# Output stage of a diffusion step's expert retrieval: the low part of V of odd experts on GpSimd, that of even ones on VectorE

## The reference, cut to what matters

```
def expert_block(args):                      # idx, g: the 128 chosen experts of a token and their gates
    hx, ix, gx = args
    act = jax.nn.gelu(jnp.einsum('tkd,td->tk', u_tab[ix], hx))
    return jnp.einsum('tk,tkd->td', gx * act, v_tab[ix])
...
x = x + g2 * peer(h, *peer_w)
y = rmsnorm(x, lnf_w)
```

## Time and profile before

| | us |
|---|---|
| three runs | 3542.67, 3549.48, 3549.56 |
| median | 3549.48 |
| span of the profiled execution, first to last instruction | 3542.8 |
| steady part of the output stage, within it | 2476 to 3466 |
| TensorE busy, whole span | 3304.0 (93%) |
| VectorE busy, whole span | 2784.9 (79%) |
| GpSimd busy, whole span | 1444.2 (41%) |
| ScalarE busy, whole span | 1255.0 (35%) |
| gathers of the output stage (L1859), 372 | 543.1 on GpSimd |
| adding their rows (L1880), 372 | 457.1 on VectorE |

### The profile page before, as it was taken

The page is one execution under the profiler, slowest core; times in us unless marked ns, Lnnn a source line. Parts: engine busy times, 40 slices in busy tenths (PEclk is TensorE's granted clock), DMA queues, the critical chain, the costliest instruction groups (busy, mean ns, idle before and its releaser), DMA issues. The chain is left out here.

```text
span 3542.8 us, 50319 instructions
## 1 busy us (share of the span) xinstructions
PE 3304.0 (93%) x17854; PEld 2976.8 (84%) x17854; DVE 2784.9 (79%) x4757; ACT 1255.0 (35%) x2299; POOL 1444.2 (41%) x950
## 2 busy tenths in 40 slices
PE   5999969699799999999699999997999999999997
PEld 2989959554799999999699999997888888888886
DVE  4555237597477799999888888884799999999998
ACT  2331135333322222222577777773222222222221
POOL 0000012111111377787555555542455655555550
PEclk8999979899899999999899999998999999999999
DMA  5235324542111377777699999996999999999993
GB/s 183 93 131 175 113 88 153 192 137 89 49 38 40 121 264 234 241 254 252 250 381 345 345 344 346 345 332 246 328 366 375 365 366 359 378 361 365 371 362 157
DMA packets 379005, 880.27 MB, mean 248 GB/s; under 512 B 32530, under 2 KB 198946, under 8 KB 375682
## 3 DMA queue, kind: packets, MB, share of 16 engines
q1 hardware_dynamic: 256004, 390.58, 33.6%
q0 software_dynamic: 115600, 423.31, 32.2%
q10 hardware_dynamic: 7280, 65.01, 4.6%
HBM read 740.61 MB, written 138.18 MB: 248 GB/s over the span
## 5 line engine op out<-in xcount | busy, mean ns | idle before, releaser
L1859 POOL DMA_INDIRECT hT<-peer_v,hT x372 | 543.1, 1460 | 448.8 <-DVE hrow L1880 333.9
L1719 PE MATMUL ps<-h_hi,u_hi 128*128 128x384 f32 x2048 | 696.0, 340 | 23.0 <-POOL u_lo L1601 15.2
L1719 PE MATMUL ps<-h_lo,u_hi 128*128 128x384 f32 x2048 | 686.7, 335 | 0.0
L1719 PE MATMUL ps<-h_hi,u_lo 128*128 128x384 f32 x2048 | 686.4, 335 | 0.0
L1982 PE MATMUL ps<-v_hi,a_hi 128*128 128x512 f32 x1536 | 599.4, 390 | 22.9 <-DVE ga_rest L1897 20.5
L1982 PE MATMUL ps<-vw_rest,a_hi 128*128 128x512 f32 x1536 | 599.0, 390 | 0.0
L1982 PE MATMUL ps<-v_hi,ga_rest 128*128 128x512 f32 x1536 | 599.0, 390 | 0.0
L1880 DVE SCALAR_TENSOR_TENSOR hrow<-hT,dots,hrow 128x1024 f32<-128x1024 f32 x372 | 457.1, 1283 | 0.0
L1719 PEld LDWEIGHTS ps<-h_hi,u_hi 128*128 128x128 f32 x2048 | 386.7, 189 | 26.0 <-issue 24.4
L1597 POOL DMA_INDIRECT hT<-u_rows,hT x212 | 329.5, 1554 | 172.7 <-DVE dots L1622 125.2
L1719 PEld LDWEIGHTS ps<-h_lo,u_hi 128*128 128x128 f32 x2048 | 386.7, 189 | 0.0
(11 more groups left out here) (335 smaller groups left out, 5839.2 us busy)
## 6 DMA issues: line engine op xcount, KB each, us to landing
uw<-u_T SPq DMA_DIRECT2D x128, 512.0 KB, 4.5
vw<-peer_v SPq DMA_DIRECT2D x128, 512.0 KB, 8.9
s_d<-so SPq DMA_DIRECT2D x256, 192.0 KB
gates_d<-big ACTq DMA_DIRECT2D x24, 2048.0 KB, 10.0
gt<-gates_d SPq DMA_DIRECT2D x32, 1536.0 KB, 28.5
ga<-s_d SPq DMA_DIRECT2D x128, 384.0 KB, 9.9
wmr<-w_modT SPq DMA_DIRECT2D x32, 512.0 KB, 4.1
tok_d<-st SPq DMA_DIRECT2D x54, 216.0 KB, 4.1
```

The source lines that it names most:

```text
L1719: mm = pe.matmul(g.ps[4 + 2 * s + b][:, 0:HALF], u[s][:, k, :], h[:, k, b * HALF:(b + 1) * HALF], start=(k == 0 and i == 0), stop=(k == KD ...
L1859: pool.indirect_dma_start(rows[n % NU], None, g.v_rows, bass.IndirectOffsetOnAxis(ap=g.pick[m % GT][:, m // GT:m // GT + 1], axis=0)).then ...
```

## The change

Of the odd experts below 120 (LATE), v_lo is subtracted by GpSimd; VectorE keeps it for even experts and for 121, 123, 125 and 127. The one semaphore v_lo_ready becomes two, v_lo_even and v_lo_odd. GpSimd does experts 1 and 3 first, ahead of all gathers; each later one goes ahead of the gather whose number is 4 over the count of rows that VectorE has added when it comes to that expert (`rows_before(e) + 4`), and it waits there for v_hi of the expert. VectorE's other work keeps its order.

```diff
+def rows_before(e):
+    if e <= 4:
+        return 0
+    j, k = (e - 5) // 4, (e - 5) % 4
+    before = (SHARE[0] if k >= 1 else 0) + (sum(SHARE[1:3]) if k == 3 else 0)
+    return min(VO * (sum(SHARE) * j + before) // STEPS, VO)
...
+    LATE = NE - 2 * BL
...
         def _(pool):
+            def low(e):
+                pool.wait_ge(v_hi_ready, e + 1)
+                pool.tensor_tensor(v_lo[e % RING][:], vw[e % RING][:], f(v_hi[e % RING][:]), ALU.subtract).then_inc(v_lo_odd, 1)
+            lows = {}
+            for e in range(1, LATE, 2):
+                lows.setdefault(min(rows_before(e) + 4, VO), []).append(e)
+            for e in range(1, BL + 1, 2):
+                low(e)
+                lows[4].remove(e)
             pool.wait_ge(a_ready, BL + 1)
             for n in range(VO):
+                for e in lows.get(n, ()):
+                    low(e)
                 m = V1 + n
...
-                dve.wait_ge(v_hi_ready, e + 1)
-                dve.tensor_tensor(v_lo[s][:], vw[s][:], f(v_hi[s][:]), ALU.subtract).then_inc(v_lo_ready, 1)
+                if e % 2 == 0 or e > LATE:
+                    dve.wait_ge(v_hi_ready, e + 1)
+                    if e % 2:
+                        dve.wait_ge(v_lo_odd, e // 2)
+                    dve.tensor_tensor(v_lo[s][:], vw[s][:], f(v_hi[s][:]), ALU.subtract).then_inc(v_lo_odd if e % 2 else v_lo_even, 1)
...
-                pe.wait_ge(v_lo_ready, j * BL + (k + 1))
+                pe.wait_ge(v_lo_odd if k % 2 else v_lo_even, j * (BL // 2) + (k // 2 + 1))
...
-                pe.wait_ge(v_lo_ready, NE)
+                pe.wait_ge(v_lo_even, NE // 2)
+                pe.wait_ge(v_lo_odd, NE // 2)
```

More of the change, by code:

```diff
@@ L1792, in outputs @@
         v_loaded, a_loaded, row_loaded, g_loaded = psem("vl"), psem("al"), g.ou_rows, psem("gl", 2)
-        v_hi_ready, v_lo_ready, a_ready, a_hi_ready, a_lo_ready = (sem(n) for n in ("vhi", "vlo", "a", "ahi", "alo"))
+        v_hi_ready, a_ready, a_hi_ready, a_lo_ready = (sem(n) for n in ("vhi", "a", "ahi", "alo"))
+        v_lo_even, v_lo_odd = sem("vlo_even"), sem("vlo_odd")
         bank_done, bank_read, tile_done = sem("bank"), sem("read"), sem("tile")
@@ L1859, in _ @@
                 pool.indirect_dma_start(rows[n % NU], None, g.v_rows, bass.IndirectOffsetOnAxis(ap=g.pick[m % GT][:, m // GT:m // GT + 1], axis=0)).then_inc(row_loaded[n % NU], 16)
+            assert max(lows) < VO
             pool.wait_ge(added, VO)
```

## The result

The changed kernel takes **3735.2 us** in the median of 4 runs (3731.2 to 3738.1), the kernel before 3547.5 us (3542.7 to 3549.6): ratio 1.0531, 95% interval 1.0516 to 1.0546. That is 188 us slower. The forecast was slower by 134 us, 3684 us, range 3603 to 3716: the direction and the kind of loss were right, the time lies 19 us above the range.

A forecast was written before the change was run, and what follows sets the result against it. TensorE bounds the output stage. VectorE's stops and late gathers lengthen each of 29 periods from 32.6 to 37.3 us, +136 us, less 1.8 us of room, +134; on the 3549.48 us median that gives 3684 us, range 3603 to 3716.

The forecast's parts named there:

- The bound: In the output stage TensorE never idles; VectorE has 1.8 us of room per period, so relieving it can't shorten the stage.
- rival C: Faster: half of 12.9 ns per matmul is due to VectorE's reads and given back, 27 us, 3522 us; chance 0.03.
- What the removal saves: Each subtraction taken off VectorE gives 0.16 us, 0.32 us a period, since the low part of a needs ScalarE's a_hi.
- The stop: VectorE's two-input instructions stand still beside GpSimd's subtraction, 2.19 us twice a period; VectorE's period becomes 34.8 us.
- the forecast's signs of being wrong: VectorE's instructions keeping 0.95 and 1.28 us beside GpSimd's subtraction, or TensorE's piece of the chain remaining whole.
- Rival A's half "stops alone": VectorE stops but gathered rows land in time: 34.8 us a period, +62 us, 3612 us; chance 0.25 for both halves.
- The gathers: Gathers queued behind GpSimd's subtraction for expert 4(j+1)+3 land late; VectorE waits 1.9 us for row 7 or 3.1 for row 8.
- From V to G: From end of v_hi, expert 4(j+1)+3, to end of a_lo, next block's first expert: 20.7 us (eight rows), 23.1 (nine).
- From G to the next V: From a_lo of a block's first expert to v_hi of its last odd expert: VectorE's work and one stop, 15.3 us.
- the clock: TensorE, idle 4.7 us each period, might be granted under 1.00, adding time; left out because no row showed it.
- Rival A's other half: Rows land late but VectorE does not stop: 2.2 us late on average, about +64 us; chance 0.25 for both halves.
- Rival B: All absorbed: stops fall on VectorE's waits for TensorE and a_hi, and gathers keep ahead; 3549 us; chance 0.07.

The follow-up runs named there:

- Run 7: Against the kernel before: the low part of odd experts left out on both engines, TensorE multiplying v_hi instead; 3544.1 us, ratio 0.9995.
- run 2: The changed kernel with each subtraction ahead of the gather 8 rows past the count instead of 4, so no gather is held; 3582.4 us, ratio 1.0097.
- run 10: The changed kernel with each subtraction ahead of the gather 6 rows past the count instead of 4; 3598.5 us, ratio 1.0160.
- run 4: The changed kernel with only expert 4j+3 of each block subtracted on GpSimd, 4j+1 back on VectorE; 3723.2 us, ratio 1.0493.
- run 6: The kernel with only expert 4j+3 on GpSimd, plus 14 useless matmuls a period in TensorE's gap; 3679.5 us, ratio 1.0381.
- run 1: The kernel before, with GpSimd only waiting for v_hi of odd experts 5 to 119 ahead of the same gathers, subtracting nothing; 3562.7 us, ratio 1.0047.
- run 5: The kernel before with GpSimd only waiting, for v_hi of odd experts but for a_lo at expert 4j+3, about 3 us later; 3733.0 us, ratio 1.0515.
- run 11: The changed kernel with only expert 4j+3 on GpSimd, its subtraction 8 rows past the count instead of 4; 3544.5 us, ratio 1.0000.

## What the prediction had right, and the step at which it was too low

**The bound.** TensorE's unbroken chain meant that relief of VectorE is worth nothing. Run 7 shows it, and rival C (faster) is out: the pace stays 884 in 200 us with VectorE busy for 176.

**What the removal saves.** The forecast said 0.16 us, since a_hi takes the subtraction's place. VectorE's wait of 0.9 us for ScalarE, 60 times, is that, and gated without a subtraction takes 2.74 us (2942.97 to 2945.71 in the changed kernel) against 2.87, 0.13 us less.

**The stop.** 2 x 2.19 us a period was forecast. The stop at expert 4(j+1)+1 was that (rows of 3.43 instead of 1.27 us); the one at V cost VectorE 1.1 us, since its rows began at V + 4.0 (before V + 2.96, forecast V + 5.0). There the gate product kept its 0.95 us, one of the forecast's signs of being wrong, and went ahead of the subtraction; a_lo was held instead, and part of that stop fell on the wait for a_hi. Rival A's half "stops alone" was priced at +62 and measured in run 2 at +38 for this reason. The sentence of the GPSIMD Engine Reference of the Trainium skill, section Key points, that GpSimd contends with VectorE instructions with two SBUF inputs, fits; the traces show it as a full stop of the one that comes second, and that VectorE's additions from PSUM (one input in SBUF) kept their 0.68 us beside a subtraction (8 of them, run 10).

**The gathers.** This is the step that failed, in size and not in kind: the times at which the held gathers go out. "The gather of row 4 is issued at V + 2.4 + 0.15 = V + 2.55" measured V + 3.45, 0.9 us later, since the subtraction took 3.22 us, not 2.4: the forecast stopped VectorE for GpSimd, but not GpSimd for VectorE. The next gather goes out another 1.8 us later, at V + 5.25, where "row 5 is issued about then" meant V + 3.7, and rows 6 and 7 follow at V + 6.5 and V + 7.8. From issue to landing these took 7.6, 9.0 and 10.2 us, about the 7.8, 8.8 and 10.1 us of the earlier trace rows. So "row 5 lands at V + 11.8, row 6 at 14.0, row 7 at 16.6, row 8 at 19.0" measured 12.9, 15.5, 18.0 and 20.4 on average: as far apart as forecast, 1.1 to 1.5 us later. (In the period shown above the waits for rows 5, 6 and 7 end at V + 13.3, 16.3 and 18.7.) From V to G the forecast had 16.6 + 4.1 = 20.7 with eight rows and 23.1 with nine, 22.0 on average; measured were 22.2 and 24.5, and 23.6 in the mean of all.

**From G to the next V** 15.3 us were forecast and 15.57 measured, but by two roads at once: VectorE with its second stop (15.19 us at a clock of 0.99 to 1.00, run 2) and TensorE at a lower clock (11.7 us for the 42 matmuls instead of 9.5). The forecast named the clock and left it out. In this stretch it was worth at most 0.4 us a period in the changed kernel, yet it holds the loss up: with only one stop the time hardly falls (run 4, +179, 15.40 us from G to V), because TensorE's road is as long; with one stop and the gap filled it is 13.67 us (run 6). It also put off the next loads, from a forecast V + 3.7 to V + 6.0, since the 84 matmuls from G to the release of the slots took 21.2 us, not 19.0.

**The sum.** Forecast 37.3 us a period, measured 39.2; the difference of 1.9 us is 1.6 in V to G and 0.3 in G to V. Over 29 periods it is 55 us, and 134 + 55 = 189 against a measured 188. The range ended at 38.4 us a period, nine rows in each, with the landing times as given: it let the rounding of rows vary and left issue and landing without an upper bound. (Its lower end, 36.0 us a period, gives 3646 us by the forecast's own sum, not 3648; nothing hangs on it.)

**Rival A's other half**, "data alone and no stop", was priced at about +64. It depends wholly on how long the gathers are held: +18 us where they wait for v_hi (run 1), +186 us where they wait 3 us longer (run 5). So the late gathers alone, with the gap of TensorE and the lower clock that follow from them, are enough for the whole loss, and the stops, which alone cost 38 us, add nothing measurable on top. That was not seen: the two were added in the forecast, while in fact each hides the other's share, the stop at V under the waits for rows and the other beside TensorE's slow matmuls. Rival B (all absorbed) holds only for run 11.

**Open.** How the DMA engines share their time between the gathers and the loads was not tried by itself. The forecast counted the landings from the first load; with the loads at V + 6.0 instead of V + 3.7 the rows landed neither 2.3 us later nor sooner after their issue than in the earlier trace rows. Why 3 us more of holding cost 4.1 us from V to G (run 1 against run 5) is put down to this sharing, which is argued, not shown.

## What to carry to other kernels

Look at what is queued behind the moved instruction before looking at what it relieves: here a subtraction of 2.4 us stood, with a wait, in front of transfers that had run up to 8 slots ahead, and 3 us more of lateness (run 5 against run 1) made each period 6 us longer. Where an engine does nothing but start transfers, work for it goes in after the free slots have been filled (8 rows ahead, not 4), and only if the engine it relieves is one that others wait for. And a gap of an engine that was full before can be paid twice, in idle time and in slow matmuls after it (run 6), unless another engine is as late (run 2 beside the changed kernel).

## What the runs showed of the hardware that was not expected

A subtraction on GpSimd and a VectorE instruction with two inputs in SBUF exclude each other in both directions: GpSimd 3.02 or 3.22 instead of 2.37 us when it came second, VectorE 2.16 or 3.15 instead of 0.95 us when it did; an addition from PSUM kept its 0.68 us. After gaps of TensorE of 2.9 to 5.6 us, from start to start, the next 42 matmuls took 11.0 to 12.5 us instead of 9.5, in the period shown with a granted clock of 0.70 over 4 us; 14 matmuls without any use, put into that gap, made one kernel 44 us faster. And a gather of 128 rows lands in 11.1 us in the median here (10.1 in the kernel before), of 128 half rows in 7.0, so that not quite two fifths of it goes away with half the bytes.
